# A two-layer transformer kernel whose first stage gets another order: weights behind each chunk's modulation tiles, eight TensorE units a chunk, token norms as a column

## The reference, cut to what matters

```python
def rms_norm(x, g):
    x32 = x.astype(jnp.float32)
    y = x32 * lax.rsqrt(jnp.mean(x32 * x32, axis=-1, keepdims=True) + EPS)
    return (y * g.astype(jnp.float32)).astype(x.dtype)
def adaln(cond, w, b):
    return jnp.split(jax.nn.silu(cond) @ w + b, N_MOD, axis=-1)
...
sh1, sc1, g1, sh2, sc2, g2 = adaln(cond_lat, w_ada[i], b_ada[i])
h = modulate(rms_norm(x, norm_mix_g[i]), sh1, sc1)
csh1, csc1, ... = adaln(cond_ctx, w_ada[i], b_ada[i])
hc = modulate(rms_norm(ctx, norm_mix_g[i]), csh1, csc1)
q, k, v = jnp.split(t @ w_qkv, 3, axis=-1)      # t = h and t = hc
```

## Time and profile before

| | us |
|---|---|
| median of three runs (lowest, highest) | 2547.7 (2546.64, 2549.43) |
| span of the profiled execution, first to last instruction | 2544.7 |
| PE busy, share of that span | 2512.1, 99% |
| DVE, ACT busy | 1621.3 (64%), 1250.3 (49%) |
| DMA queue q1, share of 16 engines' span | 62.1% |

### The profile page before, as it was taken

How to read it: one execution, slowest core, us unless ns; L and a number is a source line. 1 busy time by engine, 2 the same in 40 slices (tenths; PEclk the granted TensorE clock), 3 DMA queues, 4 the chain that set the end, 5 groups by cost and what they waited for, 6 DMA issues and landing times.

```text
span 2544.7 us, 34507 instructions
## 1 busy us (share of the span) xinstructions
PE 2512.1 (99%) x13608; PEld 2130.9 (84%) x13608; DVE 1621.3 (64%) x2365; ACT 1250.3 (49%) x1897; POOL 144.6 (6%) x148
## 2 busy tenths in 40 slices
PE   6999999999999999999999999999999999999999
PEld 2688899998888888888888898988888888888887
DVE  3567787886588886566665666665555554545554
ACT  3244433334465554355554555555566665544443
POOL 1001100000001110001110000001000000000000
PEclk9999999999999999999999999999999999999999
DMA  9953777775569885566665465556554555555555
GB/s 335 340 182 113 239 244 241 244 248 183 208 192 274 265 257 195 193 189 189 191 189 190 163 178 174 174 166 186 172 163 150 160 169 186 182 190 186 187 189 165
DMA packets 459104, 511.42 MB, mean 201 GB/s; under 512 B 36771, under 2 KB 327682, under 8 KB 458432
## 3 DMA queue, kind: packets, MB, share of 16 engines
q1 hardware_dynamic: 455936, 501.11, 62.1%
q0 software_dynamic: 2864, 8.11, 1.1%
q10 hardware_dynamic: 144, 0.02, 0.0%
HBM read 506.93 MB, written 2.22 MB: 200 GB/s over the span
## 4 chain that ended last, share of the span: by engine, by line
PE 94%; ACT 2%; DVE 1%; SPq 1%; issue 1%; DMA 1%; DVEq 0%; ACTq 0%
PE PG L925 17%; PE PG L927 17%; PE PG L926 17%; PE PG L915 13%; PE PG L918 6%; PE PG L934 4%; PE PG L936 4%; PE PG L935 4%; PE PS L1039 1%; PE PS L830 1%; SPq L745 1%; PE PG L846 1%; PE PS L1103 1%; ACT wh L1178 1%; PE PG L848 1%
## 5 line engine op out<-in xcount | busy, mean ns | idle before, releaser
L1573 DVE TENSOR_TENSOR wl<-raw,wh 128x1024 fp32r<-128x1024 f32 (+1 forms) x745 | 911.2, 1227 | 699.2 <-ACT wh L1178 697.4
L1178 ACT ACTIVATE wh<-raw 128x1024 fp32r<-128x1024 f32 (+1 forms) x745 | 786.2, 1057 | 863.5 <-PE PG L927 575.6
L915 PE MATMUL PG<-FHL,wh 128*128 128x512 f32 x1376 | 430.7, 396 | 2.4 <-DVE UP L1829 1.5
L925 PE MATMUL PG<-wh,HHL 128*128 128x512 f32 x832 | 331.2, 398 | 0.1
L927 PE MATMUL PG<-wl,HHL 128*128 128x512 f32 x832 | 324.8, 390 | 0.0
L926 PE MATMUL PG<-wh,HHL 128*128 128x512 f32 x832 | 324.1, 390 | 0.0
L918 PEld LDWEIGHTS PG<-FHL,wl 128*128 128x128 f32 x1376 | 256.2, 188 | 59.6
L918 PE MATMUL PG<-FHL,wl 128*128 128x256 f32 x1376 | 267.9, 278 | 0.0
L915 PEld LDWEIGHTS PG<-FHL,wh 128*128 128x128 f32 x1376 | 210.8, 189 | 5.2 <-issue 3.7
L927 PEld LDWEIGHTS PG<-wl,HHL 128*128 128x128 f32 x832 | 156.2, 188 | 33.6
L926 PEld LDWEIGHTS PG<-wh,HHL 128*128 128x128 f32 x832 | 156.5, 188 | 30.6
(11 more groups left out here) (402 smaller groups left out, 4216.4 us busy)
## 6 DMA issues: line engine op xcount, KB each, us to landing
raw<-in_w_in SPq DMA_DIRECT2D x208, 512.0 KB, 3.4
raw<-in_w_up SPq DMA_DIRECT2D x344, 256.0 KB, 3.4
raw<-in_w_ada SPq DMA_DIRECT2D x128, 512.0 KB, 5.1
raw<-in_w_down SPq DMA_DIRECT2D x84, 512.0 KB, 4.0
raw<-in_w_qkv SPq DMA_DIRECT2D x80, 512.0 KB, 4.6
first<-in_w_ada SPq DMA_DIRECT2D x78, 256.0 KB, 6.8
raw<-in_w_o SPq DMA_DIRECT2D x32, 512.0 KB, 3.7
raw<-in_w_in SPq DMA_DIRECT2D x64, 256.0 KB, 3.0
```

Source lines behind the costliest of these rows:

```text
L915: pe.matmul(to, hi[:, 128 * j:128 * j + 128], flat(FHL[:, step.k, :, :]), start=step.first, stop=False, skip_group_check=True)
L925: pe.matmul(dst, xh[:, cols], hi, start=step.first and j % per == 0, stop=False, skip_group_check=True)
L1178: ac.activation(wh[n % NSPL][:, 0:src.shape[1]], src, ACT.Copy).then_inc(S["hi"], 1)
L1573: dv.tensor_tensor(wl[n % NSPL][:, 0:x], src, wh[n % NSPL][:, 0:x], ALU.subtract).then_inc(S["lo"], 1)
```

## The change

In `plan`, a chunk's two weight tiles come right behind its eight modulation tiles, with none of the next chunk's ahead of them. PE does only chunk 0's eight `chunk` steps at first. `early(c)` is cut into eight units (four of six k products each, then the four v groups), and the next chunk's eight `chunk` steps stand ahead of and between the units: 1, 2, 2, 1 and 2 tiles ahead of units 0 to 4, none ahead of units 5 to 7 (`AHEAD`). The pieces rows, mod and split of the next chunk are spread over units 4 to 7. X and the context come in four loads each, and each squaring waits for its own part. The inverse root of the norms is computed on a column of 128 x 4 numbers; PE then spreads it to 128 rows with four products with the identity (phase 3) and ACT copies that to `RX` (phase 4), both behind step `chunk` 5.

```diff
+AHEAD = (1, 2, 2, 1, 2, 0, 0, 0)
...
         plan = []
         for c in range(NCH):
-            tiles, n = chunk_tiles(c), 5
-            plan += tiles[:n] + (mats[2 * c - 2:2 * c] if c else []) + tiles[n:]
-        plan += mats[KC - 2:KC]
+            plan += chunk_tiles(c) + mats[2 * c:2 * c + 2]
         self.start = len(plan)
         late = [t for n in (3, 4, 2) for half in range(2) for t in ada_tiles(n * D + half * ADA_W)]
...
         self.idle("norm", 10)
+        for n in range(8):
+            self.chunk(n)
         for c in range(NCH):
-            for n in range(8 * c, 8 * c + 8):
-                self.at["chunk", n, 0] = len(self.steps)
-                self.steps.append(Step("chunk", n))
-                if c and n % 8 == 7:
-                    self.early(c - 1)
-        self.early(NCH - 1)
+            n = 8 * c + 8
+            for unit, tiles in enumerate(AHEAD):
+                for _ in range(tiles if c < NCH - 1 else 0):
+                    self.chunk(n)
+                    n += 1
+                self.at["early", c, unit] = len(self.steps)
+                self.steps.append(Step("early", c, k=unit))
         for p, (name, g, k0, nk, tiles) in enumerate(self.prods):
             k = 0
...
         P.put(("norm", n + 1, 0), 0, "energy", x, 1)
+    for phase, at in enumerate((("norm", 9, 0), ("norm", 9, 0), ("norm", 9, 0), ("chunk", 5, 0), ("chunk", 5, 0))):
+        P.put(at, 0, "rx", 0, phase)
+
+    def mods(at, ch):
+
+        for phase in range(2):
+            for z in "xc":
+                P.put(at, 0, "mod", (z, ch), phase)
+
+    at = ("chunk", 7, 0)
     for phase in range(3):
-        P.put(("norm", 9, 0), 0, "rx", 0, phase)
+        P.put(at, 0, "rows", 0, phase)
+    P.put(at, 0, "split", 0, 0)
+    mods(at, 0)
+    P.put(at, 0, "split", 1, 0)
+    mods(at, 1)
     for c in range(NCH):
-        at = ("early", c - 1, 0) if c else ("chunk", 8 * c + 7, 0)
-        for phase in range(3):
-            P.put(at, 0, "rows", c, phase)
-        for ch in (2 * c, 2 * c + 1):
-            for z in "xc":
-                P.put(at, 0, "mod", (z, ch), 0)
-            for z in "xc":
-                P.put(at, 0, "mod", (z, ch), 1)
-        if c < NCH - 1:
-            P.put(("chunk", 8 * c + 10, 0), 0, "split", 2 * c + 1, 0)
-        else:
-            P.put(("early", c, 0), 0, "split", KC, 0)
+        if c:
+            P.put(("early", c, 0), 0, "split", 2 * c + 1, 0)
         for j in range(4):
-            P.put(("early", c, 1), 0, "v_part", (c, j), 0)
-            if c == NCH - 2 and j in (1, 3):
-                P.put(("early", c, 1), 0, "split", 2 * c + 2 + j // 2, 0)
-    at = ("early", NCH - 1, 1)
+            at = ("early", c, 4 + j)
+            P.put(at, 0, "v_part", (c, j), 0)
+            if c < NCH - 1 and j == 0:
+                for phase in range(3):
+                    P.put(at, 0, "rows", c + 1, phase)
+            if c < NCH - 1 and j in (0, 2):
+                for z in "xc":
+                    P.put(at, 0, "mod", (z, 2 * c + 2 + j // 2), 0)
+            if c < NCH - 1 and j in (1, 3):
+                for z in "xc":
+                    P.put(at, 0, "mod", (z, 2 * c + 2 + j // 2), 1)
+            if j == 1:
+                P.put(at, 0, "split", 2 * c + 2, 0)
+    at = ("early", NCH - 1, 7)
     for g in range(2):
         P.put(at, 0, "k_out", g, 0)
...
     RX = at("RX", [128, 512], F32, 190)
-    RV = [at(f"RV{i}", [128, 512], F32, 180 + 2 * i) for i in range(2)]
+    RXC = at("RXC", [128, 3, 4], F32, 180)
...
         w = Waits(sp)
-        sp.dma_start(X[:, :, :], I["xT"].rearrange("(c p) t -> p c t", p=128)).then_inc(S["xload"], 16)
-        sp.dma_start(XC[:, :, :], I["ctxT"].rearrange("(c p) t -> p c t", p=128)).then_inc(S["cload"], 16)
+        for z, dst, src in (("x", X, I["xT"]), ("c", XC, I["ctxT"])):
+            for j in range(4):
+                part = src[512 * j:512 * j + 512, :].rearrange("(c p) t -> p c t", p=128)
+                sp.dma_start(dst[:, 4 * j:4 * j + 4, :], part).then_inc(S[f"{z}load{j}"], 16)
         for i, (kind, name, k, nk, segs) in enumerate(plan):
             j = P.slot_before[i]
...
 
-        def early(c, half):
-
-            if c == 0:
-                w.wait_ge(S["rx"], 1)
+        def early(c, unit):
+
             k0, k1 = 2 * c, 2 * c + 1
-            k = k1 if half else k0
-            w.wait_ge(S["lo"], k + 1)
-            w.wait_ge(*mod_done("x", k))
-            w.wait_ge(*mod_done("c", k))
-            hi, lo = wh[k % NSPL], wl[k % NSPL]
-            for j in range(4):
-                dst, cols = PG[j // 2][:, j % 2, :], slice(128 * j, 128 * j + 128)
-                pe.matmul(dst, hi[:, cols], XHL[:, 0, k, :], start=k == 0, stop=False, skip_group_check=True)
-                pe.matmul(dst, hi[:, cols], XHL[:, 1, k, :], start=False, stop=False, skip_group_check=True)
-                end = pe.matmul(dst, lo[:, cols], XHL[:, 0, k, :], start=False, stop=k == KC - 1, skip_group_check=True)
-                if k == KC - 1 and j % 2:
+            if unit < 4:
+                k = k0 + unit // 2
+                w.wait_ge(S["lo"], k + 1)
+                w.wait_ge(*mod_done("x", k))
+                w.wait_ge(*mod_done("c", k))
+                hi, lo = wh[k % NSPL], wl[k % NSPL]
+                for j in range(2 * (unit % 2), 2 * (unit % 2) + 2):
+                    dst, cols = PG[j // 2][:, j % 2, :], slice(128 * j, 128 * j + 128)
+                    pe.matmul(dst, hi[:, cols], XHL[:, 0, k, :], start=k == 0, stop=False, skip_group_check=True)
+                    pe.matmul(dst, hi[:, cols], XHL[:, 1, k, :], start=False, stop=False, skip_group_check=True)
+                    end = pe.matmul(dst, lo[:, cols], XHL[:, 0, k, :], start=False, stop=k == KC - 1,
+                                    skip_group_check=True)
+                if k == KC - 1:
                     end.then_inc(S["early"], 1)
-            if not half:
                 return
-            for j in range(4):
-                n, dst, cols = 4 * c + j, PS[1 + j % 2], slice(128 * j, 128 * j + 128)
-                if n >= 2:
-                    w.wait_ge(S["v_sum"], n - 1)
-                for k in (k0, k1):
-                    hi, lo = (x[k % NSPL][:, 512:1024] for x in (wh, wl))
-                    pe.matmul(dst[:, :], XHL[:, 0, k, cols], hi, start=k == k0, stop=False)
-                    pe.matmul(dst[:, :], XHL[:, 1, k, cols], hi, start=False, stop=False)
-                    end = pe.matmul(dst[:, :], XHL[:, 0, k, cols], lo, start=False, stop=k == k1)
-                if j < 3:
-                    end.then_inc(S["v_pe"], 1)
-            end.then_inc(S["used"], 2)
+            j = unit - 4
+            n, dst, cols = 4 * c + j, PS[1 + j % 2], slice(128 * j, 128 * j + 128)
+            if n >= 2:
+                w.wait_ge(S["v_sum"], n - 1)
+            for k in (k0, k1):
+                hi, lo = (x[k % NSPL][:, 512:1024] for x in (wh, wl))
+                pe.matmul(dst[:, :], XHL[:, 0, k, cols], hi, start=k == k0, stop=False)
+                pe.matmul(dst[:, :], XHL[:, 1, k, cols], hi, start=False, stop=False)
+                end = pe.matmul(dst[:, :], XHL[:, 0, k, cols], lo, start=False, stop=k == k1)
+            if j < 3:
+                end.then_inc(S["v_pe"], 1)
+            else:
+                end.then_inc(S["used"], 2)
 
         def operands(name, k):
...
-                pe.matmul(PS[1][:, :], ones[:, :], AR[1][:, :], start=True, stop=True).then_inc(S["energy"], 1)
+                for b in range(4):
+                    end = pe.matmul(PS[1][:, b:b + 1], AR[1][:, 128 * b:128 * b + 128], ones[:, 0:1], start=b == 0,
+                                    stop=b == 3, skip_group_check=True)
+                end.then_inc(S["energy"], 1)
+            elif (job, phase) == ("rx", 3):
+                w.wait_ge(*const_done)
+                w.wait_ge(S["rx_col"], 1)
+                for b in range(4):
+                    end = pe.matmul(PS[2][:, 128 * b:128 * b + 128], RXC[:, 1, b:b + 1].to_broadcast([128, 128]), ident[:, :],
+                                    start=b == 0, stop=b == 3, skip_group_check=True)
+                end.then_inc(S["rx_row"], 1)
             elif (job, phase) == ("rows", 1):
                 w.wait_ge(*const_done)
...
                     w.wait_ge(S["energy"], n - 1)
-                w.wait_ge(S["xload" if z == "x" else "cload"], 16)
+                w.wait_ge(S[f"{z}load{j}"], 16)
                 ac.activation(NT[n % 2][:, :, :], norm_source(z, j), ACT.Square).then_inc(S["energy_sq"], 1)
             elif (job, phase) == ("rx", 0):
                 w.wait_ge(S["energy"], 8)
                 ac.activation(AR[1][:, :], PS[0][:, :], ACT.Copy).then_inc(S["energy_row"], 1)
+            elif (job, phase) == ("rx", 4):
+                w.wait_ge(S["rx_row"], 1)
+                ac.activation(RX[:, :], PS[2][:, :], ACT.Copy).then_inc(S["rx"], 1)
             elif (job, phase) == ("rows", 0):
```

(12 more changed lines are left out.)

## The result

The changed kernel took 2562.2 us (median of four runs, 2560.9 to 2562.4), the kernel before 2547.5 beside it: 14.8 us slower, ratio 1.0056, 95% interval 1.0044 to 1.0068. Forecast were 12.5 us more, 2560.2. The span of the profiled execution grew from 2544.7 to 2560.0 us, by 15.3. In every run on record with both numbers the time lies 1.8 to 2.2 us above the span, so the 3.0 us between the median and the span before were about 2 around the span and about 1 by which that execution was quicker than the median. In the 40 slices the first one holds 7 tenths of PE instead of 6: the start was indeed filled better, and the kernel still got slower.

What follows compares the result with a forecast made beforehand. DMA sets the pace until 47.06 us, then PE bounds the stage. Terms -10.2 + 17.9 + 1.5 + 2.0 + 1.3 give +12.5 us: span 2557.2, median 2560.2; range 2550 to 2567.

Steps and rivals of the forecast that it cites:

- The earlier start: Start of the first stage: unit 0 of `early(0)` begins at 36.85 instead of 47.06 us, -10.2 us.
- The interleaving: Tiles between k products on PE: 34 excursions at 1.19 us against six lots at 3.77, +17.9 us.
- Rows of chunk 1: Behind unit 4 in chunk 0: PE waits while ACT's v copy precedes its row copy, +1.5 us, once.
- The last chunk: Chunk 7: no interleaved tiles cover DVE's queue, so unit 2 waits for `wl` of tile 15, +2.0 us.
- The clock: Unit 0 and what follows, to about 39.5 us: low clock after sparse PE work, +1.3 us.
- Norms and loads: DVE's norm chain held nothing up, and six more load issues on SP cost nothing: 0 us.
- the nearly free interleaving: Rival: tiles pass between k products at 0.43 us each without drain, 2542 us, faster; chance 0.09.
- The late data: Rival: late first weights or mod pieces, or DVE's queue holding up unit 2: +16 to +18, 2565 us; chance 0.12.

Runs made afterwards that it cites:

- the second profile: The changed kernel run once more, unaltered, for another profile and time: 2561.0 us, +13.4 to the kernel before.
- pairs: Changed kernel with the next chunk's tiles in lots of 0, 2, 2, 2, 2 ahead of units 0 to 4 instead of 1, 2, 2, 1, 2: 2558.5 us.
- the lot ahead of unit 4: Changed kernel with all eight tiles of the next chunk in one lot ahead of unit 4: 2558.5 us, ratio 1.0040.

## Why the prediction was right

It forecast slower by 12.5 us; it was 14.8, well within the range, and the terms are found where it had put them. Step by step, in the profiled execution, where the stage ends 14.4 us later:

- **The earlier start**: -10.2 forecast, -10.2 measured (36.84). The agreement to 0.01 us is luck: the second profile has 37.88, the variants up to 38.7, mostly according to when chunk 0's last tile has landed and its rows begin. That landing was taken over unchanged from the earlier trace rows (30.05); PE began on the tile 0 to 1.6 us later in these profiles. From the rows to the first product the forecast had about 5.0 us (31.89 to 36.85), and seven of the eleven profiles have 4.85 to 4.88.
- **The interleaving**: +17.9 forecast. By the after profile it is seven periods of 17.88, less the first tile's 1.20, plus 10.93 for the bare last chunk, against 116.83 before: 125.16 - 1.20 + 10.93 - 116.83 = +18.1. The excursion costs 0.98 to 1.00 and 0.2 for the late products around it, 1.20, against 1.19 forecast. An estimate of how the +18.1 divide, from 0.33 a border and 0.86 for a set of up to two tiles: 27 more borders than with one lot in each of seven chunks, 8.9 us; six more sets, since 13 are only half filled, 5.2; and the tiles of chunk 1, which PE did before 47.06 in the old order, 3.8. The last part is work moved and not added, and every version here pays it. So the earlier start can bring no more than about 6.4 us net, 10.2 less 3.8, which the prediction does not set apart. Its remark that the sum would be 11 us less without the borders leaves out that the six old lots had one each; it is about 9.
- **Rows of chunk 1**: +1.5 forecast, 1.3 measured by the wait; the experiment that takes it away gave 3.4 with what hangs on it.
- **The last chunk**: +2.0 forecast, 2.0 measured, 0.55 at unit 0 and 1.4 at unit 2 with the late products around each wait. The place and the releaser were right. The step reckoned with DVE's queue alone; taking two sums out of it brought one sum's length, because ACT's queue was right behind.
- **The clock**: +1.3 forecast, mis-sized. It was 1.4 at the first units and 1.6 more near 54 us, behind the wait in chunk 0. The step counted only the sparse time before unit 0. These 1.7 us more are nearly all of the 1.9 by which the sum is short of the stage's 14.4. Their size is not fixed: in the second profile the start is 1.0 us later, the low clock costs 2.1 us in one stretch, and the stage ends at 178.63.
- **Norms and loads**: 0 forecast. In the changed kernel as it is none is found. But the reason given, that twelve operations on 512 columns had not held anything up, does not carry over to the new order: there they cost 1.0 us in one profile.

Of the rivals, the nearly free interleaving would have needed less than 0.82 us an excursion; it was 1.20. (At 3.57 / 8 = 0.45 us a tile its 55 tiles come to 24.5 us and not to 23.6, which changes little.) The late data did not come: behind the rows of chunk 0, PE's only wait for a load to the end of the stage is the one of 2.7 us ahead of tile 0, which lay before unit 0 as forecast.

What the border's cost comes from is only in part shown. The Trainium skill, TensorEngine Tiling (Array Packing), Key Properties, says that changing the tiling mode drains the TensorE. The runs fit that, three changes there and back fewer being worth 1.1 us, and the rule speaks for the forecast, not against it as the prediction puts it. But they do not single it out. On the way in, the first narrow product starts 0.32 us behind the last wide one, where the small products of the rows, with all 128 columns, start 0.23 behind it (71.86 to 72.09 in pairs): this part goes with the narrow form. On the way out, the slow first product and the late second one stand just as well behind the small products of the rows and behind a bare wait (0.48 to 0.50 us), where no mode changes. No run has wide float32 tiles in place of narrow ones, which would tell the two apart.

## What to carry to other kernels

Before work is cut into pieces to fill a gap, read the cost of the border from the trace, here 0.33 to 0.37 us for each excursion from 128-column to 32-column products and back, and whether half of a piece still uses the whole width: a lone tile took as long as a pair. Filling the first 10 us cost 18 in the 120 that followed. The start did not even need the pattern: with one lot of eight a chunk, the first k product came at 37.5 and 38.1, against 36.8 and 37.9 in the changed kernel. And work moved away can uncover a wait: the lot ahead of unit 4 gained 3.5 us by itself, and 16.9 once the waits were taken out of DVE's and ACT's queues and out of chunk 0.

## What the runs showed that was not expected

- The low clock (1.2 GHz) differs between executions of the same kernel: two stretches in one profile of the changed kernel, near 38 and 55 us, one longer stretch near 39 in the other, with the same gap of PE in both, ahead of the rows of chunk 1 at 51.4 and 53.2.
- A k product behind a short wait starts slowly: 0.50 instead of 0.39 us, as behind a change of the kind of product. So PE's waits of 0.28 and 1.12 us in the last chunk cost more than their length, 0.55 and 1.4.
- The start of the first k product scatters by 1.9 us between profiles, 36.8 to 38.7, mostly with the landing of the first loads, and yet the two medians of the changed kernel lie 1.2 us apart.
